# Stick-breaking attention inside a two-layer decoder step: softplus sums by matmul against running products of sigmoids

## The reference

```
z = einsum('bqhd,bkhd->bhqk', q, k) * HD_B ** -0.5 + bias
mask = arange(Lk)[None, :] < (q_offset + arange(Lq))[:, None]
u = where(mask, log_sigmoid(-z), 0)
rev_excl = cumsum(u, axis=3, reverse=True) - u
A = where(mask, exp(log_sigmoid(z) + rev_excl), 0)
o = einsum('bhqk,bkhd->bqhd', A, v)
```

## Time and profile before

| what | value |
|---|---|
| median of 3 runs | 1499.26 us (1499.24 to 1501.3) |
| span of the profiled execution | 1497.7 us |
| TensorE busy | 1475.4 us, 99% |
| VectorE busy | 1181.5 us, 79% |
| ScalarE busy | 827.6 us, 55% |
| GpSimd busy | 333.2 us, 22% |
| granted TensorE clock | 0.999 |

### The profile page before, as it was taken

How to read it: one execution, slowest core, us unless ns; L and a number is a source line. 1 busy time by engine, 2 the same in 40 slices (tenths; PEclk the granted TensorE clock), 3 DMA queues, 4 the chain that set the end, 5 groups by cost and what they waited for, 6 DMA issues and landing times.

```text
span 1497.7 us, 33609 instructions
## 1 busy us (share of the span) xinstructions
PE 1475.4 (99%) x12928; PEld 1396.7 (93%) x12928; DVE 1181.5 (79%) x2014; ACT 827.6 (55%) x1312; POOL 333.2 (22%) x330
## 2 busy tenths in 40 slices
PE   8999999999999999999999999999999999999998
PEld 8999999989999999999998888887799999999998
DVE  7866666667898988989835888888789989898753
ACT  6554444435663645546533777777756546364543
POOL 3000000002332232232142122112233332232221
PEclk9999999999999999999999999999999999999999
DMA  6233333223767767776525555543338777778621
GB/s 191 58 87 88 88 88 88 88 87 87 160 153 171 171 153 162 180 152 151 141 86 180 188 189 196 181 156 115 100 87 174 170 161 167 165 151 185 151 85 64
DMA packets 237716, 205.83 MB, mean 137 GB/s; under 512 B 8268, under 2 KB 224404, under 8 KB 237588
## 3 DMA queue, kind: packets, MB, share of 16 engines
q1 hardware_dynamic: 151346, 147.34, 31.4%
q0 software_dynamic: 68160, 47.20, 20.4%
q10 hardware_dynamic: 18082, 9.48, 2.3%
HBM read 192.19 MB, written 11.80 MB: 136 GB/s over the span
## 4 chain that ended last, share of the span: by engine, by line
PE 95%; ACT 2%; DVE 2%; issue 1%; DMA 0%; DVEq 0%; ACTq 0%
PE acc L2909 23%; PE acc L3233 19%; PE pL L3233 13%; PE pMO L3233 13%; PE acc L3333 6%; PE acc L3170 2%; PE pL L3030 1%; PE pL L3374 1%; PE pMO L3407 1%; PE pMO L3388 1%; PE acc L3450 1%; PE acc L3467 1%; PE pMO L3099 1%; PE pMO L3394 1%; PE acc L3632 1%
## 5 line engine op out<-in xcount | busy, mean ns | idle before, releaser
L662 POOL TENSOR_TENSOR wlo<-wraw,whi 128x512 fp32r<-128x512 f32 x40 | 56.2, 1434 | 443.4 <-ACT whi L799 443.4
L2909 PE MATMUL acc<-xa_hi,whi 128*128 128x288 f32 x544 | 124.6, 310 | 0.6 <-issue 0.6
L885 ACT ACTIVATE hi<-wraw 128x1024 fp32r<-128x1024 f32 x60 | 63.7, 1062 | 104.2 <-DVE wraw L2029 104.2
L868 ACT ACTIVATE hi<-wraw 128x1024 fp32r<-128x1024 f32 x60 | 63.7, 1061 | 102.9 <-PE acc L3233 102.6
L2909 PE MATMUL acc<-xa_hi,wlo 128*128 128x288 f32 x544 | 116.2, 295 | 0.0
L2909 PE MATMUL acc<-xa_lo,whi 128*128 128x288 f32 x544 | 115.6, 294 | 0.0
L3233 PE MATMUL acc<-X_lo,hi 128*128 128x288 f32 x384 | 113.3, 295 | 0.0
L3233 PE MATMUL acc<-X_hi,lo 128*128 128x288 f32 x384 | 113.3, 295 | 0.0
L3233 PE MATMUL acc<-X_hi,hi 128*128 128x288 f32 x384 | 113.1, 294 | 0.0
L2044 DVE TENSOR_TENSOR lo<-wraw,hi 128x1024 fp32r<-128x1024 f32 x60 | 73.3, 1222 | 42.2 <-ACT hi L868 42.2
L3233 PE MATMUL acc<-H_hi,hi 128*128 128x288 f32 x336 | 99.3, 296 | 1.3 <-DVE lo L2050 1.3
(11 more groups left out here) (528 smaller groups left out, 5114.1 us busy)
## 6 DMA issues: line engine op xcount, KB each, us to landing
wraw<-in_w_up_dram SPq DMA_DIRECT2D x64, 512.0 KB, 5.7
wraw<-in_w_down_dram SPq DMA_DIRECT2D x64, 512.0 KB, 5.4
Kp<-in_cache_k_dram SPq DMA_DIRECT2D x32, 512.0 KB, 4.3
Vp<-in_cache_v_dram SPq DMA_DIRECT2D x32, 512.0 KB, 5.3
wraw<-in_w_in_a_dram SPq DMA_DIRECT2D x30, 512.0 KB, 5.5
wraw<-in_w_up_dram POOLq DMA_DIRECT2D x32, 256.0 KB, 4.9
S_even<-in_w_up_dram POOLq DMA_DIRECT2D x32, 256.0 KB, 5.8
S_odd<-in_w_up_dram POOLq DMA_DIRECT2D x32, 256.0 KB, 6.4
```

What stands on the lines that cost most here:

```text
L662: ins = pool.tensor_tensor(wlo[s][:, k:k + 2, :], wraw[s][:, k:k + 2, :], whi[s][:, k:k + 2, :].bitcast(F32), ALU.subtract)
L868: act.activation(blocks4(hi02), by_rows(G % 2)[:, 0], ACT.Copy).then_inc(piece_hi, 1)
L885: act.activation(blocks4(hi31), by_depth(G % 2)[:, 0], ACT.Copy).then_inc(piece_hi, 1)
L2909: last = pe.matmul(acc[a][:, hf, 0:HALF], w[s][:, k, a * P:(a + 1) * P], x[k][:, hf * HALF:(hf + 1) * HALF], start=(k == 0 and n == 0), st ...
```

## The change

Logits now stand with queries on partitions and keys along the free axis: `logits` uses q as the stationary and k as the moving operand. The groups become query block 3 (512 columns), query blocks 2 and 0 (384 and 128), and query block 1 (256). For each group VectorE adds the mask to the diagonal blocks in PSUM (`mask`), ScalarE reads PSUM twice for each head, for sigmoid(-z) into `fg` and sigmoid(z) into `sg` (`gates`), VectorE forms the running product of `fg` from the last key backward with one scan for each query block (`products`) and multiplies it into `sg` (`weights`). The weights then have queries on partitions, so TensorE transposes them in five batches of four blocks (`weights_transposed`) and ScalarE copies each batch out of PSUM (`at_copy`). `weighted` takes 20 products of 128 columns for 8 wide ones before. The sample sequence (`past_gates`, `past_products`, `past_weights`) and the new tokens (`new_mask`, `new_gates`, `new_products`, `new_copies`) are treated alike.

The functions `soft3`, `sp_add`, `u_high`, `u_low`, `later_sums`, `minus_later`, `later_sum_1` and `masked_bias` are gone. The copies `v_rows`, `attn_out` and `past_AT` move from VectorE to ScalarE. `values_transposed` moves behind `new_rows` and now also waits for `new_gates`. ScalarE's loop over the pairs is written out, with one activation table load in front of the attention and one behind it. The core of the diff:

```
-        GROUPS = [[(3, 0), (2, 128)], [(1, 0)], [(0, 0)]]
-        GCOL, GW = [0, 384, 768], [384, 384, 512]
+        GROUPS = [[(3, 0)], [(2, 0), (0, 3 * P)], [(1, 0)]]
+        GCOL, GW = [0, 512, 1024], [512, 512, 256]
+        DIAGONAL = [(3 * P, 4 * P), (2 * P, 4 * P), (P, 2 * P)]
...
+            def gates(j, g):
+
+                act.wait_ge(z_masked, N_G * j + g + 1)
+                cols = slice(GCOL[g], GCOL[g] + GW[g])
+                for hh in range(2):
+                    z = pL[:, hh, 0:GW[g]]
+                    act.activation(fg[:, hh, cols], z, ACT.Sigmoid, scale=-SCALE, bias=bias_neg[:, bass.ds(2 * j + hh, 1)]
+                                   ).then_inc(s_done, 1)
+                    act.activation(sg[:, hh, cols], z, ACT.Sigmoid, scale=SCALE, bias=bias_h[:, bass.ds(2 * j + hh, 1)]
+                                   ).then_inc(s_done, 1)
...
+            def new_products(j):
+
+                dve.wait_ge(n_act, 5 * j + 1)
                 wait(dve, n_pe, 2 * j)
+                dve.tensor_tensor_scan(pN[:, 0:SMP][:, ::-1], fN[:, ::-1], ones[:, 0:1].to_broadcast([P, SMP]), 1.0,
+                                       ALU.mult, ALU.mult).then_inc(n_dve, 1)
+                dve.wait_ge(n_act, 5 * j + 2)
                 dve.wait_ge(n_dve, 6 * j + 3)
+                dve.tensor_tensor(sN[:], sN[:], pN[:, 1:SMP + 1], ALU.mult).then_inc(n_dve, 1)
+                dve.tensor_scalar(dN[:], ident[:], pN[:, 0:1], None, ALU.mult).then_inc(n_dve, 1)
...
+            def products(j, g, hh):
+
+                dve.wait_ge(s_done, 12 * j + 4 * g + 2 * hh + 1)
+                for i, c0 in GROUPS[g]:
+                    n = (i + 1) * P
+                    f = fg[:, hh, GCOL[g] + c0 + 1:GCOL[g] + c0 + n]
+                    ins = dve.tensor_tensor_scan(pg[:, hh, c0:c0 + n - 1][:, ::-1], f[:, ::-1],
+                                                 ones[:, 0:1].to_broadcast([P, n - 1]), 1.0, ALU.mult, ALU.mult)
+                ins.then_inc(p_done, 1)
...
+            def weights_transposed(j, b):
...
+                pe.wait_ge(a_done, 6 * j + (1, 2, 3, 4, 6)[b])
+                for t in range(4):
+                    hh, c0 = (b % 2, GCOL[b // 2] + t * P) if b < 4 else (t // 2, GCOL[2] + t % 2 * P)
+                    last = pe.transpose(pM[:, t * P:(t + 1) * P], sg[:, hh, c0:c0 + P], ident[:])
+                last.then_inc(at_full, 1)
```

More of the change, by code:

```diff
@@ L745, in kv_low @@
                 split_low_unit(a).then_inc(kv_lo, 1)
[L747 to L765, removed]
             kv_low(0, 0)
             kv_low(0, 1)
[L769 to L776, removed]
+            with pool.Fori(1, NPAIR) as j:
+                for a in range(2):
+                    kv_low(j, a)
+            kv_low(NPAIR, 0)
             pool.wait_ge(hi_done, U_OB // 2)
             split_low_unit(1).then_inc(lo_done, 1)
-            later_sum_1(NPAIR - 1, 0)
-            later_sum_1(NPAIR - 1, 1)
             pool.wait_ge(lo_done, U_OB // 2 + 1)
@@ L1459, in pair, with past_AT @@
+            def past_AT(s):
+                wait(act, O_full, s)
+                act.wait_ge(AT_full, s + 1)
+                act.activation(ATp[:], TB, ACT.Copy).then_inc(AT_done, 1)
             def pair(j, weights_in):
                 t_copy(j + 1, 0)
-                new_soft(j)
-                softplus(j, 0)
-                softplus(j, 1)
+                gates(j, 0)
+                new_gates(j)
+                v_rows(j)
                 t_copy(j + 1, 2)
-                softplus(j, 2)
@@ new lines, in weights, with group @@
+            def weights(j, g, hh):
+                cols = slice(GCOL[g], GCOL[g] + GW[g])
+                dve.wait_ge(s_done, 12 * j + 4 * g + 2 * hh + 2)
+                dve.wait_ge(p_done, 6 * j + 2 * g + hh + 1)
+                dve.tensor_tensor(sg[:, hh, cols], sg[:, hh, cols], pg[:, hh, 0:GW[g]], ALU.mult).then_inc(a_done, 1)
+            def group(j, g):
+                for hh in range(2):
+                    products(j, g, hh)
+                for hh in range(2):
+                    weights(j, g, hh)
@@ L3339, in keys_transposed @@
             def keys_transposed(j):
-                wait(pe, B_free[0], 4 * j)
-                pe.wait_ge(kv_free, 2 * j + 1)
-                for c in range(NCH):
-                    last = pe.transpose(pL[:, 0, c * P:(c + 1) * P], kf[:, c * P:(c + 1) * P], ident[:])
-                last.then_inc(B_full, 1)
-            def values_transposed(j):
-                wait(pe, B_free[1], 4 * j)
-                wait(pe, la_done, 6 * j)
-                pe.wait_ge(q_new, 2 * j + 2)
+                wait(pe, at_free, N_AT * j)
@@ L3363, in logits, with values_transposed @@
+            def values_transposed(j):
+                pe.wait_ge(n_dve, 6 * j + 1)
+                pe.wait_ge(n_act, 5 * j + 2)
+                for c in range(NCH):
+                    last = pe.transpose(pM[:, c * P:(c + 1) * P], vf[:, c * P:(c + 1) * P], ident[:])
+                last.then_inc(rows_full, 1)
             def logits(j, g):
[L3365 to L3366 removed]
                 if g == 0:
                     pe.wait_ge(kq_lo, 2 * j + 2)
[L3369 to L3371 removed]
+                    wait(pe, s_done, 12 * j)
+                else:
+                    pe.wait_ge(s_done, 12 * j + 4 * g)
+                for i, c0 in GROUPS[g]:
+                    w = (i + 1) * P
+                    for m, (q, k) in enumerate(((qhi, khi), (qhi, klo), (qlo, khi))):
@@ L3379, in later_sums @@
[L3379 to L3396 removed]
+                last.then_inc(z_full, 1)
@@ new lines, in weighted @@
+                pe.wait_ge(vr_done, j + 1)
+                for i in (3, 2, 0, 1):
+                    for kb in range(i + 1):
+                        for hh in range(2):
+                            rows = slice(64 * hh, 64 * hh + 64)
+                            b, t = {3: (hh, kb), 2: (2 + hh, kb), 0: (2 + hh, 3), 1: (4, 2 * hh + kb)}[i]
+                            last = pe.matmul(pO[rows, i * P:(i + 1) * P], vr[:, kb, rows], At[b][:, t * P:(t + 1) * P],
+                                             start=(kb == 0), stop=(kb == i))
@@ L3480, in pair @@
                 keys_transposed(j)
-                values_transposed(j)
-                new_rows(j)
-                if not first:
+                logits(j, 0)
+                if first:
+                    past_values(0)
+                else:
                     past_finish(j)
                 fill(0, 1)
-                if first:
-                    past_values(0)
                 t_fill(j + 1, 0)
-                logits(j, 0)
+                new_rows(j)
                 if first:
```

622 lines of the change are left out of this document (225 added, 397 removed).

## The result

The changed kernel takes **1517.97 us** (median; 1517.5 to 1518.28), the one before 1499.25 in the same rounds: ratio 1.0125, 95% interval 1.011 to 1.0139. It is slower, as forecast, but by 18.7 us instead of 3.5, and outside the range of 1492 to 1511.

What follows compares the result with a forecast made beforehand. TensorE bound the old kernel; after the change its freed 3.1 us per pair become waits of some 3.7. Pair 0 +0.9, six steady pairs +0.6 each (33.9 us) and last pair -0.9 sum to +3.6: 1502.8 us, range 1492 to 1511.

Steps and rivals of the forecast that it cites:

- The walk up to `past_logits` 0: Steady pair: VectorE's queue from `t_copy` 1 (3.85) takes 11.93 us to `new_out`'s end; TensorE waits, resuming at 15.9.
- GpSimd loses two small steps and keeps the splits: GpSimd's work throughout the attention pairs: two small steps go, the splits stay, with no time added to the sum.
- elsewhere cover holds: TensorE behind `past_logits` 0: beyond 0.2 us for `kv_copy`, no waits; e.g. 3.7 us covered by 6.2 ahead of `past_transposed`.
- the fills: TensorE behind `past_logits` 0 in each pair: ten fills take 8.0 us, a fill 0.8.
- `weighted` in 20 pieces: TensorE's `weighted` in each pair, cut into 20 products: same columns, 2.3 us, bounds 2.2 to 4.4.
- Pair 0: First pair: logits 0 waits for `k_low` and `q_low`, then the same 11.9 and 18.0 us follow: +0.9 us.
- The last pair: Final pair, `keys_transposed` to projection part (0,7): VectorE's queue with `ob_low` woven in, TensorE there at 29.0: -0.9 us.
- The stretch is dearer: Rival: VectorE's stretch costs more than its rows, 0.5 to 0.9 us more per pair: 1506 to 1509, or 1513; chance 0.23.
- The stretch is shorter: Rival: scans run like ordinary instructions, seven pairs win 1.2 us each: 1490, anything up to 1499; chance 0.16.
- TensorE stays the bound: Rival: TensorE's freed 3.1 us per pair show whole, 1477; needs VectorE's stretch 8.4 instead of 11.9; chance 0.07.
- The clock falls: Rival: TensorE at half clock for the 17.8 us behind the wait, seven pairs 125 us more, 1625; chance 0.02.
- The two table loads: ScalarE: two loads of 1.28 us lie in idle stretches of 12.47 and 3.20, so cost nothing.

Runs made afterwards that it cites:

- The kernel with all edits: Changed kernel plus GpSimd's split behind group 2, earlier pair start, earlier `new_products`, `past_store` and `new_out`, and `t_fill` 6 ahead of fill step 8: 1492.05 us (0.9945).
- the other order: Changed kernel with only the last pair reordered (`ob_high`(2), `ob_low`(2), `ob_low`(3) and first transposed weights earlier): 1516.8 us (1.0115).
- the last one: New last-pair order, with VectorE's steps there ordered as in steady pairs, on top of all the earlier edits to the changed kernel: 1491.32 us (0.9943).
- the variant with both edits: Changed kernel with GpSimd's split behind group 2 and `new_out` ahead of the products of group 1: 1501.85 us (1.0014).

## Why the prediction was wrong, step by step

- **The walk up to `past_logits` 0 was right.** `t_copy` 1 starts at t = 4.01 (forecast 3.85), the stretch to the end of `new_out` takes 11.87 (11.93), TensorE goes on at 15.93 (15.9). The scan over 511 is 1194 ns, as the row of 1218 for 512 said. The waits there are 1.00, 0.55 and 1.33 rather than 0.8, a small one and 2: TensorE comes to `past_logits` 0 at 14.6 instead of 14, which costs nothing, as it waits there for VectorE.
- **The step that failed** is "GpSimd loses two small steps and keeps the splits", costed at nothing, with "elsewhere cover holds" for `past_logits` 1. The split's work is unchanged. But the scans of group 2 now lie beside it and are held for 1.9 us (3.19 against 1.26), which eats the cover of `t_copy` 7. It costs 0.88 in each steady pair; taking it away gave 0.83 of pair and 6.3 us in all.
- **A term mis-sized: the fills.** Behind `past_logits` 0 come 19.66 us, not 18.0. Waits are 1.23 of it (0.88, and 0.35 where I had 0.2 for `kv_copy`), the ten fills 8.7 where I had 8.0: one behind waits, transposes or logits takes 0.87 and more (907.91 to 908.78), two in a row 1.66 to 1.76. The 0.80 of the earlier trace rows is a fill behind `later_sums`. In the kernel before, too, a fill behind transposes takes 0.87 (884.14 to 885.01); the change takes the places behind `later_sums` away and puts transposes there. Why a fill behind them is dearer no run shows. 0.88 + 0.15 + 0.65 make the 1.7 by which a steady pair (35.60) misses the forecast of 33.9. `weighted` in 20 pieces cost what was forecast (2.33). The two fills of the kernel before, from the first product to what follows:

```profile
884.14 0.51 PE L3333 MATMUL acc<-xb_hi,whi 128*128 128x288 f32 x2
...
885.01 0.60 PE L3439 MATMUL acc<-ident,Kp 128*128 128x128 f32 x4
...
909.21 0.43 PE L3333 MATMUL acc<-xb_hi,whi 128*128 128x288 f32 x2
...
910.01 0.60 PE L3458 MATMUL acc<-ident,tlS 128*128 128x128 f32 x4
```

- **Pair 0** misses by 1.96 (+2.86 instead of +0.9) and repeats the same: `past_logits` 0 starts at 832.26, 0.4 later than forecast, and 19.65 instead of 18.0 behind it.
- **The last pair** was forecast at -0.9 and is +2.0. The logits of group 1 start at 8.3 and are done only at 9.4, where VectorE has waited 0.61 for them; the 8.4 of the forecast, read as in the steady walk, was their end. Group 1 is done at 15.1 instead of 14, group 2 at 19.3 instead of 17.8, and the samples' low part at 29.0 instead of 26. `ob_low` 0 and 1 are held by GpSimd (TensorE waits 0.77 for them), the samples' low part is held too (L2660, 1.42 beside a split from 1092.72), and the other `ob_low` steps wait behind long groups. And for 3.34 us the clock is at 0.51 (1.2 GHz, from 2.4). The kernel with all edits has the same last pair without that fall and takes 31.20: of the miss of 2.9, the clock is 0.7, and 2.2 remain, waits above all, of which the other order took 1.2 away. What the holds of `ob_low` alone cost stays open, for no run moved GpSimd's split there.
- **The rivals.** "The stretch is dearer" had the right sign and too small a size; its mechanism isn't what happened. "The stretch is shorter" was priced at 32.1 for a pair; with ordinary products for scans a pair took 34.31. "TensorE stays the bound" needed the stretch at 8.4, and with it shorter or overtaken TensorE's work would have given 31.9 for a pair, not 30.2: my lower case was too low by the fills. "The clock falls" was priced for every pair (on top of the forecast its 125 us give 1628, not 1625); it fell only in the last one. The two table loads cost nothing visible, as forecast.
- In sum over the span (+18.4, forecast +3.6): six steady pairs 10.1 more than forecast, the last pair 2.9, pair 0 2.0.

## What to carry to other kernels

When a change gives VectorE instructions with two inputs in SBUF, look at what GpSimd does at that moment and count up to the whole GpSimd instruction as a wait; a copy out of PSUM in the same place costs nothing extra. The sign to look for in the trace of before is a GpSimd step of the same shape with two lengths, here 2.54 and 2.82. An in-order queue with several hand-overs is walked to its last one: here the end of the wait at `past_logits` 0 was forecast to 0.1 us, and the loss came two hand-overs later. And where the freed engine only waits, the order of the steps decides: the change made the kernel 1.25% slower as it was put, and 0.5% faster with the same arithmetic in another order.

## What the runs showed of the hardware

- One GpSimd subtraction over 128x512 (1.26 us by itself) holds a VectorE scan over 255 elements, with both inputs in SBUF, so that it takes up to 1.75 us instead of 0.67, and is slowed itself (2.91 instead of 2.52 for two). Steps that read PSUM beside it keep their length (0.41, 0.42 and 0.68).
- The clock fell to 0.50 in the last pair for about 3.3 us in the changed kernel and in six of the variants, for some 6.8 us in the one without scans, for 4 us in the last one; in two it stayed at 1.00, as in the kernel before. The pairs with 7.17 us of waits (31.20 long) and with 6.07 (30.00) kept the clock, those with 6.39 and 6.56 lost it. In the changed kernel it fell at t = 17.3, and up to there the one with all edits has the same waits in that pair and kept it: neither the length of the waits nor what TensorE did in that pair alone decides it, and what does stays open. Each is one execution; in the others only the mean clock over the whole span is on record. The steady pairs, with 4.1 us of waits in 35.6 and some 67 transposes, kept it throughout.
- The time of the clock's fall is paid only in part: the variant with both edits lost 1.46 of busy time by it (25.50 against 24.04 in the one with all), and its last pair is 0.9 longer (32.09 against 31.20), as waits behind it shrink.
